# Turn order PSMQS instead of MPSQS in an eight-expert MoE layer: a double turn first, the single 128-slot turn third

## The reference, cut to what matters

```python
def moe_swiglu(h, router_w, w1, w3, w2):
    logits = (h @ router_w).astype(jnp.float32)
    top_v, top_i = lax.top_k(logits, TOP_K)            # TOP_K = 2
    top_p = jax.nn.softmax(top_v, axis=-1)
    comb = jnp.sum(jax.nn.one_hot(top_i, N_EXPERTS, dtype=jnp.float32) * top_p[..., None], axis=-2).astype(h.dtype)
    y = jnp.zeros_like(h)
    for e in range(N_EXPERTS):
        y = y + comb[..., e:e + 1] * swiglu(h, w1[e], w3[e], w2[e])
    return y
# in reference(): x = x + g_f * moe_swiglu(hf, router_w[j], moe_w1[j], moe_w3[j], moe_w2[j]), then rmsnorm(x, norm_out)
```

## Time and profile before

| | |
|---|---|
| median of three runs | 1897.21 us |
| the profiled execution | 1895.47 us, span 1893.6 us |
| mean granted TensorE clock | 0.969 of full speed |
| TensorE busy | 1764.3 us (93% of the span) |
| VectorE, ScalarE busy | 853.6 us (45%), 690.6 us (36%) |
| GpSimd busy | 3.5 us, in six instructions |
| read from HBM | 477.03 MB, 252 GB/s over the span |
| chain that ended last | TensorE 68%, DMA 15%, VectorE 7%, ScalarE 4%, SyncE's queue 3% |

### The profile page before, as it was taken

The page is one execution under the profiler, slowest core; times in us unless marked ns, Lnnn a source line. Parts: engine busy times, 40 slices in busy tenths (PEclk is TensorE's granted clock), DMA queues, the critical chain, the costliest instruction groups (busy, mean ns, idle before and its releaser), DMA issues.

```text
span 1893.6 us, 28155 instructions
## 1 busy us (share of the span) xinstructions
PE 1764.3 (93%) x11488; PEld 1312.9 (69%) x11488; DVE 853.6 (45%) x1197; ACT 690.6 (36%) x893; POOL 3.5 (0%) x6
## 2 busy tenths in 40 slices
PE   5899899999999988998979999999989999998987
PEld 2568677888887878977867887775536887763433
DVE  2524433534533466567538985554203565420011
ACT  3323532222224545445357864454003454400001
POOL 0000000000000000000000000000000000000000
PEclk8899999999999999999979999999999999999998
DMA  8654166533731232121138979999999999999995
GB/s 319 248 197 147 43 216 229 188 100 123 244 96 61 89 91 87 47 81 42 67 134 284 376 287 398 408 409 409 408 409 405 400 408 407 408 408 409 409 409 237
DMA packets 161843, 479.96 MB, mean 253 GB/s; under 512 B 14976, under 2 KB 58160, under 8 KB 155568
## 3 DMA queue, kind: packets, MB, share of 16 engines
q1 hardware_dynamic: 161712, 478.14, 66.7%
HBM read 477.03 MB, written 1.05 MB: 252 GB/s over the span
## 4 chain that ended last, share of the span: by engine, by line
PE 68%; DMA 15%; DVE 7%; ACT 4%; SPq 3%; issue 2%; DVEq 0%; ACTq 0%
PE ps L641 16%; PE ps L643 15%; PE ps L642 15%; DMA arena<-in_moe_up 5%; PE ps L1374 4%; DMA arena<-in_moe_w 4%; DMA raw<-in_moe_up 3%; PE ps L1445 3%; SPq L590 3%; DMA raw<-in_moe_w 3%; DVE w_lo L1924 3%; PE ps L655 2%; PE ps L1363 1%; PE ps L1195 1%; PE ps L679 1%
## 5 line engine op out<-in xcount | busy, mean ns | idle before, releaser
L1924 DVE TENSOR_TENSOR w_lo<-raw,w_hi 128x1024 fp32r<-128x1024 f32 x242 | 293.9, 1223 | 353.2 <-ACT w_hi L1538 349.4
L1538 ACT ACTIVATE w_hi<-raw 128x1024 fp32r<-128x1024 f32 x242 | 253.3, 1056 | 445.5 <-PE ps L643 351.7
L641 PE MATMUL ps<-h_hi,w_hi 128*128 128x512 f32 (+1 forms) x736 | 284.8, 387 | 15.6 <-DVE h_lo L2018 10.8
L642 PE MATMUL ps<-h_hi,w_lo 128*128 128x512 f32 (+1 forms) x736 | 277.4, 377 | 0.0
L643 PE MATMUL ps<-h_lo,w_hi 128*128 128x512 f32 (+1 forms) x736 | 277.3, 377 | 0.0
L1924 DVE TENSOR_TENSOR w_lo<-arena,w_hi 128x1024 fp32r<-128x1024 f32 x144 | 173.9, 1223 | 101.5 <-ACT w_hi L1538 96.7
L1538 ACT ACTIVATE w_hi<-arena 128x1024 fp32r<-128x1024 f32 x144 | 152.3, 1060 | 128.4 <-DMA arena<-in_moe_up 65.0
L641 PEld LDWEIGHTS ps<-h_hi,w_hi 128*128 128x128 f32 x736 | 142.4, 193 | 59.6 <-issue 35.2
L643 PEld LDWEIGHTS ps<-h_lo,w_hi 128*128 128x128 f32 x736 | 141.8, 193 | 25.6
L642 PEld LDWEIGHTS ps<-h_hi,w_lo 128*128 128x128 f32 x736 | 142.6, 194 | 23.7 <-issue 0.5
L641 PE MATMUL ps<-w_hi,s_hi 128*128 128x512 f32 x336 | 134.9, 401 | 4.6 <-DVE s_lo L2447 2.4
(11 more groups left out here) (357 smaller groups left out, 2269.1 us busy)
## 6 DMA issues: line engine op xcount, KB each, us to landing
arena<-in_moe_up SPq DMA_DIRECT2D x256, 512.0 KB, 11.3
raw<-in_moe_up SPq DMA_DIRECT2D x192, 512.0 KB, 11.1
arena<-in_moe_w SPq DMA_DIRECT2D x128, 512.0 KB, 13.8
raw<-in_moe_w SPq DMA_DIRECT2D x96, 512.0 KB, 14.6
arena<-in_w_ada SPq DMA_DIRECT2D x36, 1024.0 KB, 5.1
raw<-in_ffn_w SPq DMA_DIRECT2D x66, 512.0 KB, 5.8
raw<-in_w_in_odd SPq DMA_DIRECT2D x40, 512.0 KB, 3.5
scratch<-in_w_ada SPq DMA_DIRECT2D x12, 1024.0 KB, 5.9
```

What stands on the lines that cost most here:

```text
L641: pe.matmul(dst, s_h, m_h, start=start, stop=False, **kw)
L642: pe.matmul(dst, s_l, m_h, start=False, stop=False, **kw)
L1538: act.activation(w_hi[:, o % R, :], src, ACT.Copy).then_inc(hi_done, 1)
L1924: dve.tensor_tensor(w_lo[:, o % R, :], src, w_hi[:, o % R, :].bitcast(F32), ALU.subtract).then_inc(lo_done, 1)
```

## The change

The order becomes `PSMQS` and a last S. The columns follow: the P turn now has expert 0 (column 0) as its wide expert and column 4 as its narrow one; S has column 3, M column 2, Q columns 1 and 6, and the last two turns columns 5 and 7. So each kind keeps its widths of slots, and the number of units, their size and the work on each stay as they are. Around this:

- The first 12 wide units of the P turn come first in the load list, then eight narrow ones. Units 12, 13 and 14 of the wide expert do not go through the ring at all: they have places of their own (`EXTRA`, in `X_ACC` and `X_Y`) and a semaphore of their own (`extra_in`).
- SyncE's wait for `routed` stands after 12 ring loads and the three extra ones.
- VectorE sorts the experts, reorders the columns and makes the narrow expert's one-hots at once, before `gather_lo(0)`, and gives out the sorted numbers as soon as they are there (`routed` 1); the numbers on overflow come later (`routed` 2), and what needs them waits for 2.
- TensorE does the first wide block of four units, gathers the narrow expert's tokens (`gather_s(0)`), and goes on with the second wide block and then eight narrow units. ScalarE copies that gather out (`gathered_s`) in step 3 of the turn.
- GpSimd sets `acc` to zero after the 15th wide unit has been split, as two of the extra units lie there until then.

```diff
-KINDS = "MPSQS"
-M_COL = {0: 0, 1: 2, 3: 1}
-S_COL = {1: 4, 2: 3, 3: 6, 4: 5, 5: 7}
+KINDS = "PSMQS"
+M_COL = {0: 0, 2: 2, 3: 1}
+S_COL = {0: 4, 1: 3, 3: 6, 4: 5, 5: 7}
+FIRST = 12
+EXTRA = {FIRST: X_ACC, FIRST + 1: X_ACC + UNIT, FIRST + 2: X_Y}
...
-    units = []
+    units = [(0, "m", v) for v in range(FIRST)] + [(0, "s", v) for v in range(8)]
...
-                units += [(tau, part, v + k) for k in range(4)]
+                units += [(tau, part, v + k) for k in range(4)
+                          if tau or not ((part == "m" and (v < FIRST or v + k in EXTRA)) or (part == "s" and v < 8))]
...
+        def split_from(o):
+
+            n = M_ORDER[o - U_MOE]
+            if n is None:
+                return ar(EXTRA[o - U_MOE], UNIT), (extra_in, 16 * len(EXTRA))
+            return moe_slot(n), moe_seen(n)
...
-                if n == EXP_UNITS:
+                if n == FIRST:
+                    for w, at in EXTRA.items():
+                        sp.dma_start(ar(at, UNIT), expert_unit(w)).then_inc(extra_in, 16)
                     sp.wait_ge(routed, 1)
...
+                if tau == 0:
+                    m_group(0, 0)
+                    gather_s(0, S_BANK[kind])
+                    m_group(0, 1)
                 if has_s:
 
                     pe.wait_ge(sx_g, tally(s, 1, 1))
-                for cb in range(CB):
+                if tau == 0:
+                    for w in range(2):
+                        s_group(0, w)
+                for cb in range(1 if tau == 0 else 0, CB):
...
-            pool.wait_ge(rlo_done, HEADS)
+            pool.wait_ge(lo_done, U_MOE + max(EXTRA) + 1)
...
+                    if tau == 0 and v == 3:
+                        gathered_s(0, S_BANK[kind])
...
                 link(dve.tensor_copy(order[:, 7:8], idx[:, 0, 3:4]))
+                dve.tensor_copy(trips[:, T_EXPERT:T_EXPERT + N_EXP], order[:, 0:N_EXP]).then_inc(routed, 1)
...
             one_hots(0)
+            route_sort()
+            route_columns()
+            one_hots_s(S_COL[0], 0)
             gather_lo(0)
...
-                    if tau == 0 and v == 10:
-                        route_sort()
-                    if tau == 0 and v == 14:
-                        route_columns()
```

More of the change, by code:

```diff
@@ L195 @@
 S_AT = {(tau, v): n for n, (tau, part, v) in enumerate(UNITS) if part == "s"}
-M_ORDER = [M_AT[tau, v] for tau in range(FIXED) if KINDS[tau] != "S" for v in range(EXP_UNITS)]
+M_ORDER = [M_AT.get((tau, v)) for tau in range(FIXED) if KINDS[tau] != "S" for v in range(EXP_UNITS)]
 def splits_by(tau, v):
@@ L1287, in moe_turn @@
                 if both:
-                    places = {2: (4, 8)}[len(steps)]
+                    places = {0: (), 2: (4, 8)}[len(steps)]
                 else:
@@ L1323, in x_unit, with m_group, s_group @@
                     return moe_slot(M_AT[tau, v])
+                def m_group(cb, w):
+                    bank = (cb % 2, 2)[w] if both else 2 * (cb % 2) + w
+                    v = 8 * cb + 4 * w
+                    for k in range(4):
+                        hi, lo = m_unit(v + k)
+                        for kk in range(2):
+                            kt = 2 * k + kk
+                            g = slice(2048 + kt * P, 2048 + (kt + 1) * P)
+                            i = three(ps[:, bank, :], s_hi[:, g], s_lo[:, g], hi[:, kk * BANK:(kk + 1) * BANK],
+                                      lo[:, kk * BANK:(kk + 1) * BANK], kt == 0, kt == KT - 1)
+                        i.then_inc(pe_used, 1)
+                        if not both:
+                            old_outputs(v + k + 1)
+                def s_group(cb, w):
+                    bank, at = (3, 256 * w) if both else (2 * (cb % 2) + w, 0)
+                    v = 8 * cb + 4 * w
+                    for k in range(4):
+                        src = s_unit(v + k)
+                        for kk in range(2):
+                            kt = 2 * k + kk
+                            for j in range(2):
+                                i = pe.matmul(ps[64 * j:64 * j + 64, bank, at:at + 256], ar(X_G + kt * HALF, HALF),
+                                              src[:, kk * BANK + 256 * j:kk * BANK + 256 * j + 256],
+                                              start=(kt == 0), stop=(kt == KT - 1), skip_group_check=True)
+                        i.then_inc(s_used, 1)
+                        if not both:
+                            old_outputs(v + k + 1)
+                if tau == 0:
+                    m_group(0, 0)
+                    gather_s(0, S_BANK[kind])
+                    m_group(0, 1)
                 if has_s:
                     pe.wait_ge(sx_g, tally(s, 1, 1))
-                for cb in range(CB):
+                if tau == 0:
+                    for w in range(2):
+                        s_group(0, w)
+                for cb in range(1 if tau == 0 else 0, CB):
                     if cb >= 2 and has_m:
@@ L1339, in moe_turn @@
                         if has_m:
[L1340 to L1350, removed]
+                            m_group(cb, w)
                         if both and cb >= 1 and w == 0:
@@ L1367, in moe_turn @@
                         elif has_s:
[L1368 to L1380, removed]
+                            s_group(cb, w)
                         if both:
@@ L1532, in hi @@
                 else:
-                    act.wait_ge(*moe_seen(M_ORDER[o - U_MOE]))
-                    src = moe_slot(M_ORDER[o - U_MOE])
+                    src, landed = split_from(o)
+                    act.wait_ge(*landed)
                 if o >= R:
@@ L1920, in lo @@
             def lo(o):
-                src = raw[:, slot(o), :] if o < U_MOE else moe_slot(M_ORDER[o - U_MOE])
+                src = raw[:, slot(o), :] if o < U_MOE else split_from(o)[0]
                 dve.wait_ge(hi_done, o + 1)
@@ L2427, in route_trips @@
                 link(dve.tensor_reduce(cnt[:, T_EXPERT + N_EXP:].unsqueeze(2), each_over[:, 0], AX.X, ALU.add))
-                dve.tensor_copy(trips[:, :], cnt[:, :]).then_inc(routed, 1)
+                dve.tensor_copy(trips[:, T_EXPERT + N_EXP:], cnt[:, T_EXPERT + N_EXP:])
+                dve.tensor_copy(trips[:, 0:T_EXPERT], cnt[:, 0:T_EXPERT]).then_inc(routed, 1)
             def route_over():
```

9 lines of the change are left out of this document (5 added, 4 removed).

## The result

The changed kernel takes 1901.13 us (median of 20 runs, 1898.39 to 1904.18), the kernel before 1896.59 us in the same comparison: a ratio of 1.0027, 95% interval 1.0020 to 1.0033. It is slower by 0.27%, where 5.1 us less were forecast. Its profiled execution took 1900.59 us, with a span of 1898.8 us (before 1895.47 and 1893.6), at a granted clock of 0.97 (0.969).

The account below looks back on a forecast made before the run. The load stream at 408 GB/s bounds the kernel; 13.6 us lost at the start plus 16.4 at the handover minus 35.1 recoverable gives -5.1, so 1892.1 us; range 1882 to 1903 us, the forecast's own 1886 to 1898.

Parts of the forecast that it names:

- The start of P, 13.6 us: At the first turn, the load stream loses 13.6 us in four stalls; bounds 10 to 19 us.
- The first stall: At the start of P, load 12 waits for the sort of the experts: 4.5 us lost.
- the last two together: At the start of P, loads 34 and 39 wait for narrow units 8 and 12: 0.7 and 3.5 us lost.
- the second stall: At the start of P, load 22 waits for wide unit 8 to be split, behind the narrow gather: 4.9 us lost.
- The cover of 5.0 us: VectorE's 5.00 us wait ahead of `s_lo` hides the routing chain of some 4.2 us, so TensorE's start is not moved.
- rival 2: The first turn is bound by TensorE, the stream stops in each group: at 11.0 us a group 1905 us; chance 0.15.
- The handover from M to Q: Between the 128-slot turn and Q, the stream loses 14.2 + 1.0 + 1.2 = 16.4 us; bounds 11 and 21 us.
- T: End of the M turn on TensorE, forecast at D + 132.5 us; load 14 of Q flows at T + 7.6.
- M itself loses nothing: Inside the M turn, wide places are given up at the split, so the stream keeps 20 units of lead.
- D: The moment at which the last S unit ahead of M has landed; M's first wide unit is split at D + 3.6 us.
- The two groups without a lead: In Q's next two groups, scatters of M's results leave the lead at nothing: 1.0 us more lost.
- rival 3: The gain is eaten, both stalls near their upper bounds, 18 + 18 us: 1898 us, no change; chance 0.18.

Follow-up runs that it names:

- experiments 1 and 2: The changed kernel with its Q turn made a P turn: 1896.74 us; then the changed kernel in orders PSQMS and PMSQS: 1898.60 and 1894.10 us.
- experiments 5 and 6: The changed kernel with the double turn's gathers apart: 1897.34 us; then also earlier scatters and ten overwritten matmuls: 1897.87 us, with narrow gather first too: 1896.42 us.
- experiments 3 and 4: The changed kernel with the first narrow gather ahead of the first wide block: 1895.96 us; the kernel before with sort and columns at once: 1897.31 us.
- experiment 5: The changed kernel with the 64-slot gather two down blocks behind the 128-slot one, not right behind it: 1897.34 us.

## Why the prediction was wrong

- **Pace and account**: right, as far as one execution of each kernel can say. A unit in 1.285 us, a free order, and time lost only while the stream stands still: fourteen traces give the same remainder, to 1.4 us.
- **The start of P, 13.6 us**: right in mechanism and nearly in size. 15.4 us in the profiled run, 16.5 on the mean of seven traces (17.2 less 0.7 before the first byte). The first stall was 4.1 us for 4.5, the last two together 4.6 for 4.2. The excess is the second stall: it cost 6.8 us (4.4 in the ten microseconds from 1000 us, 2.4 in the next ten), forecast 4.9. The standstill itself, to 1011 us, was of the forecast size; the rest are dips up to 1018 us. The clock was at 0.50 from 1006 to 1008 us, and ScalarE's next two splits waited 0.29 and 0.36 us for TensorE; that this makes the dips was not tried apart. The cover of 5.0 us held; `acc` cost nothing.
- **P turn bound by TensorE (rival 2)**: false; 407 GB/s from 1040 to 1140 us, and no dip in each group. A group took 9.3 to 9.9 us of TensorE, forecast 9.6, against 10.28 of loads.
- **The handover from M to Q, 14.2 + 1.0 + 1.2 = 16.4 us**: this is the step that failed. The prediction put the return of the stream at T + 7.6, since Q's places are held (measured T + 7.7), and that part was right; the size was 25.0 us. "M itself loses nothing" was wrong: the lead of 20 units ran out at about 1380 us, and 14.6 of the 25 us were lost inside M. In this order it doesn't change the sum, because load 14 of Q has to wait for T whatever was lost before it; without Q behind M it is nearly the whole loss (experiments 1 and 2).
- **The parts of the 8.6 us missing there**: 7.8 are T, forecast at D + 132.5 and measured at D + 140.3. The parts of T, read from the trace and tried in experiments 5 and 6: half clock at the gathers, 3.4 us (3.2 gained where it was absent), where the prediction took a third of it on the ground that it had been seen once; half clock at the start of M, 1.6 us, which stood there as a rule and was not taken; the first turned block's wait for VectorE, 1.45; a seventh turn, 0.45. Some 0.9 us of T are in none of them. The other 0.8 us are a balance. D was the landing of a unit, but the stream's lead counts from its flow, which ends earlier; by difference that is some 1.8 us. The 1.2 us taken beforehand for the clock are in the measured T already and come off again. The two groups without a lead lost 1.1 to 1.3 us from 1460 to 1500 us, for 1.0. No run tried these apart.
- **The clock behind the start of M.** The Trainium skill, "TensorE: Matmul & The Clock Gate" (Part 1), says that activity releases a throttled array; by that rule the prediction would have been 2.2 us higher. The trace agrees in the direction: 1.6 us, and none with work in the wait. The fall in the busy gather this rule doesn't cover.
- **The sum** of the two errors, 1.8 at the start and 8.6 at the handover, is 10.4 us; the forecast of -5.1 became +5.2 in the span and +4.5 in the median. The kernel ended on the side of rival 3, the eaten gain, and 3 us above it, with other sizes than the 18 + 18 us it named. That 1901.13 us lies inside the wide range of 1882 to 1903 us is luck: the upper end was put there for rival 2, which is false, and the forecast's own range ended at 1898.

## What to carry to other kernels

- When a stream of loads bounds a kernel, measure what it loses, stretch by stretch, and add only that. An order that ends one loss can open another: with the turn that TensorE does slower than its loads in first place 34 us were lost there, ahead of Q 25, and about 20 in the two other places tried.
- Pair the work that is slower than its loads with work that is faster; moving it moved most of its loss along. Merging the two turns, with scatters that hardly wait, took 16 to 18 us off the kernel before by the ratios, where the change had added 5.
- Where a forecast hangs on one end time far down a chain, put the whole known cost of each wait and clock fall into it, not a third: there they all go one way.

## What the hardware showed that was not expected

- TensorE's granted clock fell to 0.50 at gathers of 64 columns while the engine was busy all the time. Ahead of Q, with both gathers together, it fell for 6.8 us in seven of ten traces (the kernel before and the change among them), for 3.4 us in one, and not at all in two (experiments 3 and 4); with the gathers apart it fell for 3.4 us in three of four and not at all in one (experiment 5). So apart the fall was no longer than half; what decides whether it comes these traces don't say.
- A wait of 2.64 us on TensorE, behind a turn in which it waited for each unit, was followed by 3.4 us at half clock in four of four traces; with ten matmuls in that wait the clock stayed at full in two of two.
